# One product in place of three for the 16 meta keys of an attention kernel

## The reference, cut to what matters

```
s = (q_nope . k_nope + q_rope . k_rope) * scale      # per head, 1024 queries x 1040 keys
p = softmax(s)
o = p @ v                                            # 1040 keys x 128 values
```

## Time and profile before

| | |
|---|---|
| time, median of 3 runs | 2174.02 us (2173.63 to 2174.09) |
| span of the profiled execution, first to last instruction | 2171.4 us |
| instructions | 30857 |
| TensorE busy | 2124.8 us, 98% of the span |
| VectorE, ScalarE, GpSimd busy | 59%, 44%, 18% |
| mean granted TensorE clock | 0.997 |
| attention stage | about 946 to 1387 us of the span |

### The profile page before, as it was taken

One profiled execution on the slowest core, in us unless ns is written; L12 is line 12 of the kernel. 1 busy time (PEld: TensorE's weight loads), 2 busy tenths in 40 slices (PEclk: granted clock), 3 DMA queues, 4 the chain that ended last, 5 costly groups with the idle time before them and its releaser, 6 DMA issues. The chain is left out here.

```text
span 2171.4 us, 30857 instructions
## 1 busy us (share of the span) xinstructions
PE 2124.8 (98%) x11536; PEld 1795.8 (83%) x11536; DVE 1282.6 (59%) x1966; ACT 948.0 (44%) x1550; POOL 397.9 (18%) x242
## 2 busy tenths in 40 slices
PE   8999999999999999999999999899999999999999
PEld 8988888888888888778888888777888888888886
DVE  3403664756647557447777777667866766651431
ACT  6314354443554535455555555545432323243422
POOL 1110000000000000021111111020065554524443
PEclk9999999999999999999999999999999999999999
DMA  5112111120120111130111111254322222354452
GB/s 188 60 54 69 35 64 53 45 68 34 63 68 34 63 52 46 49 138 1 45 45 48 47 50 47 99 186 159 135 83 81 95 78 73 124 182 165 149 182 96
DMA packets 79101, 181.82 MB, mean 84 GB/s; under 512 B 6976, under 2 KB 27776, under 8 KB 77344
## 3 DMA queue, kind: packets, MB, share of 16 engines
q1 hardware_dynamic: 79008, 180.56, 24.1%
HBM read 142.13 MB, written 38.40 MB: 83 GB/s over the span
## 5 line engine op out<-in xcount | busy, mean ns | idle before, releaser
L88 PE MATMUL h_bank<-hn_hi,w_hi 128*128 128x512 f32 (+2 forms) x952 | 371.1, 390 | 2.8 <-ACT raw L716 1.6
L90 PE MATMUL h_bank<-hn_hi,w_lo 128*128 128x512 f32 (+2 forms) x952 | 353.4, 371 | 0.0
L89 PE MATMUL h_bank<-hn_lo,w_hi 128*128 128x512 f32 (+2 forms) x952 | 353.0, 371 | 0.0
L88 PEld LDWEIGHTS h_bank<-hn_hi,w_hi 128*128 128x128 f32 x952 | 179.0, 188 | 33.3 <-issue 8.7
L90 PEld LDWEIGHTS h_bank<-hn_hi,w_lo 128*128 128x128 f32 x952 | 178.7, 188 | 27.9
L89 PEld LDWEIGHTS h_bank<-hn_lo,w_hi 128*128 128x128 f32 x952 | 179.2, 188 | 26.4 <-issue 3.8
L716 ACT COPY raw<-h_bank 128x512 f32<-128x512 f32 (+2 forms) x119 | 63.9, 543 | 279.9 <-PE h_bank L90 249.5
L2150 ACT CAST w_hi<-w_raw 128x1024 fp32r<-128x1024 f32 x79 | 82.8, 1049 | 213.2 <-PE f_bank L90 201.7
L895 DVE TENSOR_TENSOR w_lo<-w_raw,w_hi 128x1024 fp32r<-128x1024 f32 x52 | 63.5, 1221 | 138.2 <-ACT w_hi L696 138.2
L1132 POOL MEMSET ckv_hi<- 128x224 f32 x1 | 0.3, 284 | 778.8 <-POOLq L585 778.8
L1453 ACT CAST prob_hi<-a_bank 128x512 fp32r<-128x512 f32 x144 | 83.0, 588 | 130.8 <-PE a_bank L1721 130.2
(11 more groups left out here) (411 smaller groups left out, 5371.3 us busy)
## 6 DMA issues: line engine op xcount, KB each, us to landing
w_raw<-in_w_ffn SPq DMA_DIRECT2D x82, 512.0 KB, 3.7
w_raw<-in_w_hgrn SPq DMA_DIRECT2D x54, 512.0 KB, 3.2
raw_up<-in_w_ffn SPq DMA_DIRECT2D x18, 512.0 KB, 4.6
hidden<-gate_blocks SPq DMA_DIRECT2D x34, 256.0 KB, 2.0
w_raw<-in_w_out SPq DMA_DIRECT2D x15, 512.0 KB, 3.3
w_raw<-in_w_head SPq DMA_DIRECT2D x9, 512.0 KB, 6.0
X<-in_x SPq DMA_DIRECT2D x8, 520.0 KB, 9.4
values<-values_h SPq DMA_DIRECT2D x32, 128.0 KB, 1.7
```

Of the source, the lines that this page charges most:

```text
L88: pe.matmul(out, wh, xh, start=start, stop=False)
L89: pe.matmul(out, wh, xl, start=False, stop=False)
L90: return pe.matmul(out, wl, xh, start=False, stop=stop)
```

## The change

The ninth tile gets a layout of its own, by groups of 32 rows ("STACK"). The 16 meta rows of the values are loaded three times: to the ends of rows 32 to 64 (LOW_VALUES), 64 to 96 (LOW_KEYS) and 96 to 128 (TURNED). In the tile of v_hi, VectorE then overwrites the first group with the low part. On the side of the probabilities, ScalarE writes prob_hi of the turned rows into both LOW_VALUES and TURNED (two copies of 32 rows where there was one of 128), and VectorE writes prob_lo of these rows into LOW_KEYS of the same buffer. One matmul over 128 rows then gives v_lo.p_hi + v_hi.p_lo + v_hi.p_hi. Row groups in which nothing is stacked meet weights of zero.

```diff
+        STACK = 2 * META
+        LOW_VALUES, LOW_KEYS, TURNED = (slice(n * STACK, (n + 1) * STACK) for n in (1, 2, 3))
+        THREE = [slice(rows.stop - META, rows.stop) for rows in (LOW_VALUES, LOW_KEYS, TURNED)]
...
 # SP
+                        v_meta_lo.wait(sp, p, 1, lag=1)
                         sp.dma_start(v_raw[:, 0:TT, :], t.d_mv[:, 0:TT, bass.ts(hp, P)]).then_inc(v_in.sem, 16)
-                        sp.dma_start(v_raw[META_AT:P, TT, :],
-                                     t.d_mv[0:META, TT, bass.ts(hp, P)]).then_inc(v_in.sem, 16)
+                        for rows in THREE:
+                            sp.dma_start(v_raw[rows, TT, :],
+                                         t.d_mv[0:META, TT, bass.ts(hp, P)]).then_inc(v_in.sem, 16)
...
 # POOL, values(p): v_lo of 8 tiles in place of 9
-                    pool.tensor_tensor(v["lo", par][:], v_raw, v["hi", par][:].bitcast(F32), ALU.subtract
+                    pool.tensor_tensor(v["lo", par][:], v_raw[:, 0:TT, :], v["hi", par][:, 0:TT, :].bitcast(F32),
...
 # ACT, high(k); values(p) waits for 64 in place of 32
-                    act.copy(turned_hi[k % RING][:], turn_bank[k % 2][:]).then_inc(p_hi.sem, 1)
+                    for rows in (LOW_VALUES, TURNED) if k == TT else (slice(0, P),):
+                        source = TURNED if k == TT else rows
+                        last = act.copy(turned_hi[k % RING][rows, :], turn_bank[k % 2][source, :])
+                    last.then_inc(p_hi.sem, 1)
...
 # DVE, new; called in the first segment after normalize(1) (j == 2), and at the end of begin
+                def values(p):
+                    hi = v["hi", p.base % 2][LOW_VALUES, TT, :]
+                    v_hi_done.wait(dve, p, 1)
+                    dve.tensor_tensor(hi, v_raw[LOW_VALUES, TT, :], hi.bitcast(F32), ALU.subtract
+                                      ).then_inc(v_meta_lo.sem, 1)
...
 # DVE, low(k)
+                    if k == TT:
+                        dve.tensor_tensor(hi[LOW_KEYS, :], turn_bank[k % 2][TURNED, :],
+                                          hi[TURNED, :].bitcast(F32), ALU.subtract).then_inc(p_lo.sem, 1)
+                        return
...
 # PE, multiply(k), behind its wait on p_lo
+                    if k == TT:
+                        v_meta_lo.wait(pe, h, 1)
+                        pe.matmul(o_bank[:], v["hi", par][:, k, :], turned_hi[k % RING][:], start=False, stop=True
+                                  ).then_inc(pv_done.sem, 1)
+                        return
```

More of the change, by code:

```diff
@@ L1269, in attention_heads @@
         LAST = L - P
-        META_AT = P - META
+        STACK = 2 * META
+        LOW_VALUES, LOW_KEYS, TURNED = (slice(n * STACK, (n + 1) * STACK) for n in (1, 2, 3))
+        THREE = [slice(rows.stop - META, rows.stop) for rows in (LOW_VALUES, LOW_KEYS, TURNED)]
         v_raw = t.raw[:, QS * L:QS * L + TILES * P].rearrange("p (k m) -> p k m", k=TILES)
-        v = {(x, i): sb(f"v_{x}{i}", [P, TILES, P], F32R) for x in both_parts for i in range(2)}
+        v = {(x, i): sb(f"v_{x}{i}", [P, TILES if x == "hi" else TT, P], F32R) for x in both_parts for i in range(2)}
+        sb("after_values", [P, 2 * P])
         prob = [t.raw[:, 0:QS * L].rearrange("p (j k) -> p j k", j=QS), sb("prob1", [P, QS, L])]
@@ L1302, in attention_heads @@
         cleared = t.sem("attention_cleared")
-        v_in, v_hi_done, v_lo_done = signal("av_in", 32), signal("av_hi_done", 1), signal("av_lo_done", 1)
+        v_in, v_hi_done, v_lo_done = signal("av_in", 64), signal("av_hi_done", 1), signal("av_lo_done", 1)
+        v_meta_lo = signal("av_meta_lo_done", 1)
         piece_done, piece_hi, piece_read = (signal("a_piece", NP_), signal("a_piece_hi", len(BY_ACT)),
@@ L1386, in values @@
                     v_hi_done.wait(pool, p, 1)
-                    pool.tensor_tensor(v["lo", par][:], v_raw, v["hi", par][:].bitcast(F32), ALU.subtract
-                                       ).then_inc(v_lo_done.sem, 1)
+                    pool.tensor_tensor(v["lo", par][:], v_raw[:, 0:TT, :], v["hi", par][:, 0:TT, :].bitcast(F32),
+                                       ALU.subtract).then_inc(v_lo_done.sem, 1)
                 def both(p, h):
@@ L1432, in values @@
                     par = p.base % 2
-                    v_in.wait(act, p, 32)
+                    v_in.wait(act, p, 64)
                     pv_done.wait(act, p, 0, lag=1)
@@ L1571, in low @@
                     p_hi.wait(dve, h, i * TILES + k + 1)
-                    dve.tensor_tensor(turned_lo[k % RING][:], turn_bank[k % 2][:],
-                                      turned_hi[k % RING][:].bitcast(F32), ALU.subtract
+                    hi = turned_hi[k % RING]
+                    if k == TT:
+                        dve.tensor_tensor(hi[LOW_KEYS, :], turn_bank[k % 2][TURNED, :],
+                                          hi[TURNED, :].bitcast(F32), ALU.subtract).then_inc(p_lo.sem, 1)
+                        return
+                    dve.tensor_tensor(turned_lo[k % RING][:], turn_bank[k % 2][:], hi[:].bitcast(F32), ALU.subtract
                                       ).then_inc(p_lo.sem, 1)
@@ L1603, in segment @@
                             normalize(nxt, j)
+                        if j == 2 and which == 0 and p is not None:
+                            values(p)
                         if last:
@@ L1733, in multiply @@
                     p_lo.wait(pe, h, i * TILES + k + 1)
+                    if k == TT:
[3 more added lines that the diff above has]
+                        return
                     three(pe, o_bank[:], v["hi", par][:, k, :], v["lo", par][:, k, :],
-                          turned_hi[k % RING][:], turned_lo[k % RING][:], k == 0,
-                          k == TILES - 1).then_inc(pv_done.sem, 1)
+                          turned_hi[k % RING][:], turned_lo[k % RING][:], k == 0, False).then_inc(pv_done.sem, 1)
                 def segment(cur, nxt, p, which):
```

## The result

The changed kernel takes 2180.55 us (median of 6 runs, 2179.09 to 2183.36), the kernel before 2174.06 us (6 runs, 2173.58 to 2175.22). The ratio is 1.003, 95% interval 1.0018 to 1.0041: slower, by 6.5 us. The forecast was 2175.5, with a range up to 2178.2. Spans of the two profiled executions: 2177.3 and 2171.4, 5.9 us apart.

What follows compares the result with a forecast made beforehand. TensorE was taken to bound calls, a ScalarE-VectorE chain the joints between them. Terms -2.2 + 3.2 + 0.3 + 0.2 = +1.5 us took 2174.0 to 2175.5 us, range 2171.0 to 2178.2.

Steps and rivals of the forecast that it cites:

- What bounds the kernel: Attention stage: TensorE bounds the time inside a call; at each head's end a chain from ScalarE's ninth-tile copy arrives last.
- I take 0.48, since a row shows this very pair.: ScalarE's second ninth-tile copy: adds 0.48 us before `low(8)` can start; bounds 0.48 overlapped and 0.59 not.
- VectorE's other start of rows: `low(8)` on other rows than its neighbours: top_tail 0.43 to 0.49 us later, 0.46 taken; upper end adds 0.2 us in sum.
- Second segments: Seven calls: the chain to TensorE's next start comes 0.46 us later each, +3.2 us; bounds 0 and 4.2.
- First segments: Seven calls: next projections start 0.31 us earlier each, -2.2 us; bounds -3.2 and 0.
- The loads: Two more DMAs per head: hidden in the loop, +0.3 us at the start; bounds 0 and 1.2.
- VectorE's `values`: New 32-row VectorE instruction, about 0.28 us long: +0.2 us once, at the end of `begin` before k_nope_lo.
- The last head: TensorE idles for VectorE anyway; in the very last segment two matmuls less and a copy more cancel within 0.1: 0.
- Rival 3, the clock: After idleness TensorE gets half its clock: once, before the last head, 2177.2 us, 12%; at every head 2187, 5%.
- The sum: Whole kernel: first segments -2.2, second +3.2, loads +0.3, VectorE's `values` +0.2, giving +1.5 us and 2175.5 us.

Runs made afterwards that it cites:

- e3: Kernel before without the second and third matmul of the ninth tile, low parts of the meta keys' products left out: 2170.25 us (ratio 0.9985).
- e2: Kernel before with ScalarE's copy of the ninth tile split in two, rows 0 to 96 and 96 to 128, all three products kept: 2181.46 us (ratio 1.0032).
- e9: Kernel before with a second ScalarE copy of the whole ninth tile, all 128 rows, into a tile nobody reads: 2179.18 us in its one run.
- e7: Kernel before with two more loads of the 16 meta rows per head into a tile nobody reads; ScalarE waits for all: 2174.19 us (ratio 1.0004).
- e10: Kernel before with ScalarE's first fold ahead of the values at the start, and eight useless matmuls in the last head: 2170.82 us (ratio 0.9985).
- e5: Changed kernel with VectorE signalled after the first copy, and fold and VectorE's new subtraction reordered at the stage's start: 2171.98 us (ratio 0.9994).
- e6: Changed kernel with eight matmuls of no use for TensorE in the last head, where it waits for the last normalizations: 2178.28 us (ratio 1.0022).
- e8: Changed kernel with VectorE signalled after the first copy, the stage's start reordered, and eight useless matmuls in the last head: 2169.83 us (ratio 0.9982).
- e1: Changed kernel with VectorE signalled after the ninth tile's first copy, the second made from it in SBUF beside VectorE's subtraction: 2173.09 us (ratio 0.9997).

## Why the prediction was wrong

The mechanism was the right one and its place too; the sizes were too small, and the chance of 0.10 for slower was far too low. The sum had seven calls at +1.0 us, the start at +0.5 and the last head at 0; the profiles show +3.3, +1.3 and +1.3. The term that failed worst is the copy's price in the calls, as the next paragraphs show.

*What bounds the kernel.* Right. e3 shows that matmuls won in second segments are lost in waiting; e2 that a copy there is paid in full.

*"I take 0.48, since a row shows this very pair."* This is the step that failed first. The row shows two copies of 128 rows, which start at the same row. The new pair writes from rows 32 and 96 on and takes 1.17 us, not 1.07. I had 0.59 as a bound, and the row did not show the pair that it was taken for. e9 against e2 settles it: 1.07 against 1.17, and a call 0.23 us shorter. It costs 0.10 at both segments.

*VectorE's other start of rows.* Named as 0.43 to 0.49, and priced in the middle. In the changed kernel top_tail starts 0.73 us after `low(8)`, with full rows in e2 it is 0.61: 0.12 us, of which the sum held 0.03. The Trainium skill ("VectorE: DVE Perf Modes", Two Vector instructions with no wait between them) has a VectorE instruction that starts in another group of 32 rows than its forerunner held until all earlier ones have finished. The trace agrees: the next instruction starts 0.04 us after the end and not 0.08 before it.

*Second segments.* Predicted 0.46, measured 0.63: the copies 0.10 more, VectorE's start most of the rest.

*First segments.* Predicted -0.31, measured -0.17: `low(8)` comes 0.10 later by the copies and 0.04 by small gaps, and TensorE stands for it.

Both together: a call was to grow by 0.15 us and grew by 0.47; over seven calls 3.3 us in place of 1.0. A small difference of two terms that pull apart takes the errors of both: each was off by 0.15 us, and the sum by a factor of three.

*The loads.* Predicted +0.3, measured +0.60 before the second fold in the changed kernel (1.06 in place of 0.46) and +0.45 with the loads alone (e7). The row that answers to the earlier trace rows is v_hi at 957.53, when the stage starts 0.39 us earlier. Over all heads the copies land 2.8 to 3.4 us after their issue each, so they do not simply land with the large one. The Trainium skill's 2.0 us ("DMA: Bandwidth & Descriptors", Anatomy of one DMA), by which the sum would have been smaller, does not fit here: no copy landed sooner than 2.8 us. It is fitted on another path.

```profile
957.53 1.15 ACT L1441 CAST v_hi<-raw 128x1152 fp32r<-128x1152 f32 x1 [1.05 <-DMA raw<-attention_values]
...
DMA to landing us min/median/max: 2.8/3.0/3.4
```

*VectorE's `values`.* Its length was right, 0.28 us; its place costs more than the 0.2 that I took. It works on rows 32 to 64 between neighbours that start at row 0, and nothing around it overlaps:

```profile
978.10 0.76 DVE L1581 TENSOR_SCALAR raw<-raw,inv 128x1040 f32<-128x1040 f32 x1
978.89 0.28 DVE L1549 TENSOR_TENSOR v_hi<-raw,v_hi 32x128 fp32r<-32x128 f32 x1
979.20 1.04 DVE L1526 TENSOR_TENSOR k_nope_lo<-a_scores,k_nope_hi 128x384 fp32r<-128x384 f32 x2
```

k_nope_lo starts 1.10 us after the start of the last normalization, where it was 0.67 (977.59 to 978.26 in the trace of before), and TensorE waits 1.12 us where it waited 0.7: +0.43. The rest of the start's +1.33, 0.3 us, is a third wait, for ScalarE's exponential. TensorE in the changed kernel, then in the kernel before:

```profile
974.59 0.39 PE L1700 MATMUL a_bank<-k_nope_hi,q_nope_hi 128*128 128x256 f32 x1 [0.79 <-ACT raw L1450]
```

```profile
974.09 0.39 PE L1678 MATMUL a_bank<-k_nope_hi,q_nope_hi 128*128 128x256 f32 x1 [0.47 <-ACT raw L1444]
```

With the loads alone (e7) it is 0.78, which makes up the 0.75 us of that start; in e10, without them but with the fold moved, it is 0.76. So it goes with a start whose order in time has moved; what sets its length stays open.

*The last head.* Predicted 0, measured +1.34 in one profile each. From the very last `high(8)` to the next stage it is 3.67 us (1388.75 to 1392.42) where it was 3.45 (1383.41 to 1386.86): the copy and the two matmuls do not cancel, +0.2. The other part, about 1.1 us, is TensorE's clock at half for longer: 0.58 in the 8 us from 1376 on, where the kernel before has 0.79 in the 8 us from 1371 on. e7 shows that this can come without any change in the last head, so with one profile of each it can't be charged to the change.

*Rival 3, the clock.* Not at the joints between calls: with 1.12 us of idleness the granted clock of the loop stays at 1.00 there. At the joint before the last head TensorE waits 1.04 and 1.28 us, the 2.3 that rival 3 named; four profiles (e2, e5, e6, e8) show a stretch at half clock behind it, the changed kernel's own does not. Whether it came in its other timed runs no trace shows.

*The sum.* With the measured sizes: calls +3.3, start +1.3, last chain +0.2, to which the clock adds about 1.1: 5.9 in the profiles. Of the 6.5 us between the medians 0.6 are left. One timed run of the changed kernel (2183.36) had a mean granted clock of 0.995, where the others had 0.996 and 0.997, so the stretches at half clock seem to differ from run to run; how much of the median is theirs stays open. One slip changes nothing in the sum: the 0.7 us behind `begin` is one of the seven waits of the earlier trace rows, not an eighth.

## What to carry to other kernels

Before an engine that is busy for 98% is relieved, look at where it waits and follow that chain back: if its first link is an instruction that the edit doubles, the relief is worth only what lies outside the chain, and the doubling is paid in full. Two instructions of an engine on different start rows are not the pair that a row of full height shows; take the price without overlap. Where a product needs a copied operand, signal the consumer that is on the chain first and copy beside it: this alone took 7 us off the changed kernel (e1), 6 of them by the length of its calls.

## What the runs showed of the hardware

- ScalarE overlaps the tail of a copy from PSUM with the head of the next (start to start 0.48 us, 0.59 long) if both begin at the same row. With starts at rows 0 and 96 (e2), or with outputs from rows 32 and 96 on (the changed kernel), two take 1.17 us.
- VectorE does the same: 0.61 us from a subtraction of 0.69 us to the next start with equal rows (e2), 0.73 us with others (the changed kernel, e1).
- A ScalarE copy of 32x512 takes 0.58 us, of 128x512 0.59 us; a copy of 96 rows is the same.
- With eight matmuls of no use in a stretch of TensorE's waits, the granted clock was 1.00 over the 8 us in which it was 0.58 without them (e6), and a kernel that differs by them alone took 2.15 us less (e8 against e5).
